# A hybrid decoder step: input rows turned once, the roots multiplied in by feature tile, conditioning and weight blocks loaded between input tiles, and a tile's halves overlapped

## The reference, cut to what matters

```python
mod = jax.nn.silu(c) @ w_ada + b_ada
sh1, sc1, g1, sh2, sc2, g2 = (m[:, None, :] for m in jnp.split(mod, 6, axis=-1))
h = rmsnorm(x, norm_mix_w) * (1.0 + sc1) + sh1
z = h @ w_in + b_in
q_raw, f_raw, i_raw, og_raw, glu_a, glu_b, gate_a, gate_b = jnp.split(z, IN_SPLITS, axis=-1)
```

## Time and profile before

| | |
|---|---|
| median of 3 runs | 1977.72 us (1976.07 to 1977.74) |
| the profiled execution's own time | 1975.14 us |
| its span, first to last instruction | 1973.4 us |
| busy share of the span: TensorE, VectorE, ScalarE, GpSimd | 98%, 67%, 33%, 12% |
| mean granted clock of TensorE | 0.994 of full |
| moved from and to memory | 237.45 MB, 120 GB/s over the span |

### The profile page before, as it was taken

How to read it: one execution, slowest core, us unless ns; L and a number is a source line. 1 busy time by engine, 2 the same in 40 slices (tenths; PEclk the granted TensorE clock), 3 DMA queues, 4 the chain that set the end, 5 groups by cost and what they waited for, 6 DMA issues and landing times.

```text
span 1973.4 us, 39636 instructions
## 1 busy us (share of the span) xinstructions
PE 1935.4 (98%) x16182; PEld 1876.1 (95%) x16182; DVE 1316.6 (67%) x1800; ACT 655.9 (33%) x1066; POOL 232.5 (12%) x256
## 2 busy tenths in 40 slices
PE   7999999999999999998999999999999999999998
PEld 6999999999999999988989999999999999999998
DVE  6697979786878788897775665554445544465543
ACT  6212313131413222233544433333343333433332
POOL 2300000000000000021132554700000000000000
PEclk8999999999999999999999999999999999999999
DMA  8723041413232222222366644444444544444443
GB/s 254 229 61 87 24 112 45 112 45 92 66 90 67 70 77 79 78 75 93 107 216 210 187 135 139 132 138 140 136 137 143 154 136 136 135 147 148 138 133 110
DMA packets 417245, 237.45 MB, mean 120 GB/s; under 512 B 16375, under 2 KB 411287, under 8 KB 417072
## 3 DMA queue, kind: packets, MB, share of 16 engines
q1 hardware_dynamic: 416672, 234.48, 40.6%
q10 hardware_dynamic: 416, 0.72, 0.1%
HBM read 211.91 MB, written 24.11 MB: 120 GB/s over the span
## 4 chain that ended last, share of the span: by engine, by line
PE 83%; DVE 10%; ACT 3%; issue 2%; DMA 1%; DVEq 0%; POOL 0%; ACTq 0%; SPq 0%
PE Z L887 45%; PE Z L905 27%; DVE yb L1453 4%; DVE w_lo L1305 2%; PE R L980 1%; PE Z L852 1%; PE R L924 1%; ACT w_hi L1813 1%; PE R L1006 1%; PE R L930 1%; PE R L1013 1%; PE R L1015 1%; PE R L987 1%; DVE S L1420 1%; DMA w_raw<-in_w_out_dram 1%
## 5 line engine op out<-in xcount | busy, mean ns | idle before, releaser
L1813 ACT ACTIVATE w_hi<-w_raw 128x1024 fp32r<-128x1024 f32 (+1 forms) x316 | 329.4, 1043 | 932.3 <-PE Z L887 469.7
L1305 DVE TENSOR_TENSOR w_lo<-w_raw,w_hi 128x1024 fp32r<-128x1024 f32 (+1 forms) x305 | 386.0, 1266 | 369.1 <-ACT w_hi L1813 361.4
L905 PE MATMUL Z<-h_hi,w_hi 128*128 128x352 f32 x1488 | 499.7, 336 | 2.8 <-issue 1.7
L905 PE MATMUL Z<-h_hi,w_lo 128*128 128x352 f32 x1488 | 478.4, 321 | 0.0
L905 PE MATMUL Z<-h_lo,w_hi 128*128 128x352 f32 x1488 | 477.8, 321 | 0.0
L1453 DVE SCALAR_TENSOR_TENSOR yb<-up,vec,yb 128x1024 f32 (+1 forms) x240 | 327.2, 1363 | 28.8 <-DVE yb L1453 3.7
L887 PE MATMUL Z<-h_hi,w_hi 128*128 128x352 f32 x1056 | 342.1, 324 | 0.0
L887 PE MATMUL Z<-h_hi,w_lo 128*128 128x352 f32 x1056 | 339.2, 321 | 0.0
L887 PE MATMUL Z<-h_lo,w_hi 128*128 128x352 f32 x1056 | 338.6, 321 | 0.0
L905 PEld LDWEIGHTS Z<-h_hi,w_hi 128*128 128x128 f32 x1488 | 279.5, 188 | 20.2 <-issue 16.7
L905 PEld LDWEIGHTS Z<-h_lo,w_hi 128*128 128x128 f32 x1488 | 280.3, 188 | 0.5 <-issue 0.5
(11 more groups left out here) (303 smaller groups left out, 2408.8 us busy)
## 6 DMA issues: line engine op xcount, KB each, us to landing
w_raw<-in_w_ffn_in_dram SPq DMA_DIRECT2D x132, 512.0 KB, 3.8
w_raw<-in_w_in_dram SPq DMA_DIRECT2D x64, 512.0 KB, 5.0
w_raw<-in_w_out_dram SPq DMA_DIRECT2D x48, 512.0 KB, 4.2
w_raw<-in_w_ffn_out_dram SPq DMA_DIRECT2D x48, 512.0 KB, 4.0
aw<-in_w_ada_dram SPq DMA_DIRECT2D x32, 512.0 KB, 4.0
w_raw<-in_w_ffn_out_dram SPq DMA_DIRECT2D x24, 384.0 KB, 3.4
ada_w<-in_w_ada_dram SPq DMA_DIRECT2D x16, 512.0 KB, 6.2
mbuf<-merged_scratch SPq DMA_DIRECT2D x32, 176.0 KB, 4.3
```

The costliest lines, as they stand in the source:

```text
L905: last = mm(out, w[:, kt, :], x[:, kt, cols], start=kt == 0 and m == 0, stop=kt == NJ - 1 and m == 2)
L1305: st.tell(V.tensor_tensor(w_lo[b.par][:, 0:n, :], w_raw[b.par][:, 0:n, :], w_hi[b.par][:, 0:n, :].bitcast(F32), ALU.subtract), w_split, b. ...
L1813: A(w_hi[b.par][:, 0:n, :], w_raw[b.par][:, 0:n, :], ACT.Copy).then_inc(w_hi_ready, 1)
```

## The change

The roots are no longer multiplied into the rows before turning. The input is turned once, as it is; the root of each token is spread over all partitions by one small matmul per row tile (`root_row`) and kept as `rsrow` (128 x 1056), and the scaling is `xt * am * rsrow` by feature tile. The nine row tiles have a buffer each, where h_hi comes later. The copies of the turned x pass from ScalarE to VectorE. SyncE's queue has block 0, x4, conditioning 0, x5, block 1, x6, conditioning 1, x7, x8, and then conditioning 2 to 7 in four buffers. Conditioning 0 and 1 are made between the turns. In the tile loop the prompt part of h is made in two halves of 512 tokens by VectorE (scale), ScalarE (h_hi with the shift as bias) and VectorE (h_lo); the 32 sample tokens go to GpSimd. `conditioning(kt + 2)` moves behind block 0's products of tile kt, `fold_groups(kt + 2)` into block 1's. The last two tiles are made for block 0 first and then for block 1. The exponentials of the lower bounds move from the input phase into the loop.

TensorE:

```diff
+                for t in range(NC + 1):
+                    turn_tokens(t)
+                    if t >= 2:
+                        root_row(t - 2)
+                    if t == 2:
+                        vectors()
+                    if t == 4:
+                        conditioning(0)
+                    if t == 5:
+                        pe.wait_ge(const_ready, 3)
+                        fold_groups(0)
+                    if t == 7:
+                        conditioning(1)
+                for t in range(NC - 1, NC + 1):
+                    root_row(t)
+                fold_groups(1)
                 pe.wait_ge(x_evac, N_TURNS)
...
+                pe.wait_ge(row_copied, NC + 1)
+                pe.wait_ge(w_split, 2)
+                for kt, b in FIRST_STEPS:
+                    pe.wait_ge(h_ready, kt + 1)
+                    pe.wait_ge(hs_ready, kt + 1)
+                    for m, (w, x) in enumerate(((w_hi[b], h_hi), (w_hi[b], h_lo), (w_lo[b], h_hi))):
+                        for g in range(G):
+                            last = mm(Z[b][:, g, 0:GW], w[:, kt, :], x[:, kt, g * GW:(g + 1) * GW],
+                                      start=kt == 0 and m == 0, stop=kt == NJ - 1 and m == 2)
+                        if b == 1 and m == 1 and kt + 2 < NJ:
+                            fold_groups(kt + 2)
+                    if kt == NJ - 1:
+                        last.then_inc(block_done, 1)
+                    if b == 0 and kt + 2 < NJ:
                         conditioning(kt + 2)
...
+            def root_row(t):
+
+                m = tokens(t)
+                pe.wait_ge(rms_ready, t + 1)
+                wait(pe, row_copied, t - 2)
+                mm(row_bank(t), rs9[0:m, t:t + 1].to_broadcast([m, P]), ident[0:m, 0:m], start=True, stop=True) \
+                    .then_inc(row_made, 1)
```

```diff
+FIRST_STEPS = tuple((kt, b) for kt in range(NJ - 2) for b in range(2)) + tuple(
+    (kt, b) for b in range(2) for kt in range(NJ - 2, NJ))
+HALF_PROMPT = (slice(0, TP // 2), slice(TP // 2, TP))
```

VectorE (after the copies of xt and of the rows; `condition(0)` stands behind t = 7):

```diff
+            def scale_prompt(j):
                 st.settle()
...
+                for half in HALF_PROMPT:
+                    st.tell(V.scalar_tensor_tensor(hbuf[j % 3][:, half], xt[:, j, half], am[:, j, 0:1], rsrow[:, half],
+                                                   ALU.mult, ALU.mult), h_full, 2 * j + 1 + HALF_PROMPT.index(half))
+
+            def prompt_low(j):
+
+                for n, half in enumerate(HALF_PROMPT):
+                    dve.wait_ge(h_hi_ready, 2 * j + n + 1)
+                    ins = V.scalar_tensor_tensor(h_lo[:, j, half], hbuf[j % 3][:, half], mod[:, SH1 * NJ + j, 0:1],
+                                                 h_hi[:, j, half].bitcast(F32), ALU.add, ALU.subtract)
+                    st.do(ins) if n == 0 else st.tell(ins, h_ready, j + 1)
...
+                if j:
+                    condition(j)
+                scale_prompt(j)
+                prompt_low(j)
+                if j == 2:
+                    lower_bounds_in()
+                if j == 5:
+                    lower_bounds()
+            dve.wait_ge(hs_ready, NJ)
```

ScalarE:

```diff
+            def groups_out(j):
+                act.wait_ge(ada_done, j + 1)
+                A(acols[:, j % 2, :, :].rearrange("p s n -> p (s n)"), R[j % 2][:, 0:2 * P], ACT.Copy).then_inc(acols_ready, 1)
...
+                if t in (5, 8):
+                    groups_out(t // 8)
+                if t in (3, 5):
+                    hi(Idx(t // 4))
+
+            for j in range(NJ):
+                for n, half in enumerate(HALF_PROMPT):
+                    act.wait_ge(h_full, 2 * j + n + 1)
+                    A(h_hi[:, j, half], hbuf[j % 3][:, half], ACT.Identity, bias=mod[:, SH1 * NJ + j, 0:1]) \
+                        .then_inc(h_hi_ready, 1)
+                if j + 2 < NJ:
+                    groups_out(j + 2)
+                if j == 3:
                     act.wait_ge(lb_in, 1)
                     A(lbs[:, 0, :], lbs[:, 0, :], ACT.Exp)
                     A(lbs[:, 1, :], lbs[:, 1, :], ACT.Exp).then_inc(lb_exp, 1)
```

GpSimd (the splits of blocks 0 and 1 now stand ahead of the roots of row tiles 4 and 6):

```diff
+            pool.wait_ge(row_copied, NC + 1)
+            pool.wait_ge(x_evac, N_TURNS)
+            st.tell(Q.tensor_tensor(xs[:, :, :], xt[:, :, TP:T], rsrow[:, TP:T].unsqueeze(1).to_broadcast([P, NJ, TS]),
+                                    ALU.mult), xs_scaled, 1)
+
+            def samples(j):
+
+                pool.wait_ge(am_ready, j + 1)
...
+                st.do(Q.tensor_tensor(seqs(xs[:, j, :]), seqs(xs[:, j, :]), per_seq(am[:, j, 1:NSEQ]), ALU.mult))
+                st.settle()
+                st.do(Q.tensor_tensor(seqs(h_hi[:, j, TP:T]), seqs(xs[:, j, :]), shift, ALU.add))
+                st.do(Q.tensor_tensor(seqs(full), seqs(xs[:, j, :]), shift, ALU.add))
+                st.settle()
+                st.tell(Q.tensor_tensor(h_lo[:, j, TP:T], full, h_hi[:, j, TP:T].bitcast(F32), ALU.subtract),
+                        hs_ready, j + 1)
```

More of the change, by code:

```diff
@@ L325, in program @@
     ada_w = [e(f"ada_w{i}", [P, 2, 8, P]) for i in range(WADA)]
-    xrow = [e(f"xrow{i}", [P, D]) for i in range(XBUF)]
     vrow = e("vrow", [P, 4, P])
+    rsrow = e("rsrow", [P, T])
+    xs, hs = e("xs", [P, NJ, TS]), e("hs", [P, NJ, TS])
     hbuf = (ta, tb, ysum)
@@ L521, in load_mod @@
                         .then_inc(adaw_loaded[j % WADA], 16)
-            for t in range(XBUF):
+            for t in range(4):
                 load_x(t)
@@ L788, in vectors, with turn_tokens @@
                 last.then_inc(p0_done, 1)
-            def turn(t, row, normed, done, read):
+            def turn_tokens(t):
+                pe.wait_ge(x_loaded[t], 16)
                 m = tokens(t)
                 for n in range(2 * t, 2 * t + 2):
-                    wait(pe, read, n - 2)
-                    bank = turn_bank(normed, n)
+                    wait(pe, x_evac, n - 2)
+                    bank = turn_bank(n)
                     for j in range(4):
[L797 to L812, removed]
+                        c = (4 * (n % 2) + j) * P
+                        last = transpose(bank[:, j * m:(j + 1) * m], xrow[0:m, t, c:c + P], ident[0:m, 0:m])
+                    last.then_inc(x_turned, 1)
+            def root_row(t):
[4 more added lines that the diff above has]
+                    .then_inc(row_made, 1)
             def conditioning(j):
@@ L1251, in lower_bounds, with copy_row, condition @@
                 st.do(V.tensor_scalar(lbs[:, 2, :], lbs[:, 0, :], 1.0, None, ALU.subtract))
[L1253 to L1277, removed]
+            def copy_row(t):
+                dve.wait_ge(row_made, t + 1)
+                st.tell(V.tensor_copy(rsrow[:, t * P:t * P + tokens(t)], row_bank(t)), row_copied, t + 1)
+            def condition(j):
                 dve.wait_ge(folded, j + 1)
-                st.do(add_bias(SH1))
-                st.tell(add_bias(SC1), mod_read, j + 1)
+                made = R[j % 2][:, FOLD_COL:FOLD_COL + 32].rearrange("p (s n) -> p s n", n=16)[:, :, 0:NSEQ]
+                bias = vec[:, V_ADA:V_ADA + 6 * NJ].rearrange("p (s j) -> p s j", j=NJ)[:, SH1:SC1 + 1, j:j + 1]
+                st.tell(V.tensor_tensor(mod[:, :, :].rearrange("p (s j) n -> p s j n", j=NJ)[:, SH1:SC1 + 1, j, :], made,
+                                        bias.to_broadcast([P, 2, NSEQ]), ALU.add), mod_read, j + 1)
                 st.settle()
@@ L1293, in modulate @@
-                dve.wait_ge(h_hi_ready, j + 1)
-                st.tell(V.tensor_tensor(h_lo[:, j, :], buf[:, 0:T], h_hi[:, j, :].bitcast(F32), ALU.subtract), h_ready,
-                        j + 1)
-            for j in range(NJ):
-                modulate(j)
+            for t in range(NC + 1):
+                for n in range(2 * t, 2 * t + 2):
+                    dve.wait_ge(x_turned, n + 1)
+                    st.tell(V.tensor_copy(turned(xt, n), turn_bank(n)[:, 0:4 * tokens(t)].rearrange(
+                        "p (j t) -> p j t", j=4)), x_evac, n + 1)
+                if t >= 2:
+                    copy_row(t - 2)
+                if t == 3:
+                    first_evac(1, vec[:, :], R[1][:, 0:NVEC])
+                if t == 7:
+                    condition(0)
@@ L2133, in _ @@
                         rms_ready, t + 1)
-            for b in range(2):
-                low(Idx(b))
+            pool.wait_ge(row_copied, NC + 1)
[4 more added lines that the diff above has]
+                pool.wait_ge(am_ready, j + 1)
+                if j == 0:
+                    pool.wait_ge(xs_scaled, 1)
+                full, shift = hs[:, j, :], per_seq(mod[:, SH1 * NJ + j, 1:NSEQ])
+                st.do(Q.tensor_tensor(seqs(xs[:, j, :]), seqs(xs[:, j, :]), per_seq(am[:, j, 1:NSEQ]), ALU.mult))
[5 more added lines that the diff above has]
+                        hs_ready, j + 1)
+            for j in range(NJ):
+                samples(j)
             pool.wait_ge(h_ready, NJ)
```

92 lines of the change are left out of this document (26 added, 66 removed).

## The result

| | before | changed |
|---|---|---|
| median, us | 1977.73 (1976.07 to 1978.03, 6 runs) | 1988.57 (1986.22 to 1990.04, 6 runs) |
| ratio, 95% interval | | 1.0057 [1.0046, 1.0068] |
| span of the profiled execution, us | 1973.4 | 1986.8 |
| block 2 starts, us | 74.84 | 84.80 |
| mean granted clock | 0.994 | 0.992 |

A forecast was written before the change was run, and what follows sets the result against it. TensorE was taken to bound the kernel, so only the start-up counts: block 2 moves from 74.84 to 79.7 us (37.2 + 7.0 + 20.8 + 6.7, then 3.6, 1.5, 2.9), +4.9 on the median: 1982.6 us, range 1975.5 to 1986.5.

The forecast's parts named there:

- Part 2: Tile loop: ScalarE's queue order closes a loop through conditioning, 5.2 us a tile where TensorE's own work is 4.57.
- Rival C: Tile loop: ScalarE's queue doesn't bind and TensorE paces it as before; -2.6 us, 1975.1 us; chance 0.13.
- four times 5.2, and once 5.2 + 1.5: Tile loop from T(1) to T(6): four tiles of 5.2 us and one of 6.7 with table load and Exp.
- Nine more products end block 0 at 76.8: Loop's end: after T(7) at 75.3, block 0 ends at 76.8 and block 2 starts 2.9 later, at 79.7 us.
- Part 1: Input phase until T(0): x7 lands at 28.0 us, last copies end at 33.6, T(0) follows at 37.2.
- T(0): Moment when tile 0's first product can start, forecast at 37.2 us.
- rival B: Input phase: TensorE is at 2.4 GHz when x7 lands and at T(0); +0.9 us, 1978.6 us; chance 0.28.
- Rival D: Tile 0, loop and T(7): every GpSimd sample operation lands whole in VectorE's time; +3.1, 1985.7 us; chance 0.11.
- Part 3: Loop's end, from T(6) at 71.7 to block 2 at 79.7 us, with the 1.1 us stall for split weights gone.
- T(6) to T(7): From tile 6's first possible product to tile 7's: VectorE begins h(7) only at T(6), 3.6 us.

The follow-up runs named there:

- e1: Changed kernel with conditioning(kt+2) put ahead of tile kt's products again; 1978.29 us, ratio to before 1.0009.
- e7: Changed kernel's tile loop and Exp with e6's input phase (all input tiles loaded before the weights); 1981.64 us, ratio to before 1.0029.
- e3: Changed kernel with 18 unread matmuls put on TensorE into each gap, ahead of tile 4 and of tile 7's block 0 products; 1987.09 us, ratio to before 1.0053.
- e10: Changed kernel with GpSimd's sample operations held until VectorE has finished h_lo of the same tile; one execution, 2003.94 us.
- e5: Changed kernel with e1 and e2 together and the fold between a tile's two blocks as before the change; 1976.51 us, ratio to before 1.0002.
- e6: e5 with all inputs loaded before weights, conditionings 0 and 1 behind all turns, block 0 and 1 splits on VectorE; 1972.78 us, ratio to before 0.9990.
- e4: Changed kernel with blocks 0 and 1 alternating in the last two tiles as well, as before the change; 1988.03 us, ratio to before 1.0057.
- e2: Changed kernel with the two Exp and their table load moved back into the input phase; 1985.46 us, ratio to before 1.0048.

## Why the prediction was right about the sign and wrong about the size

**Part 2, the loop through ScalarE's queue: right.** Forecast 5.2 us a tile, measured 5.31, 5.30 and 5.28 for the undisturbed tiles; e1 shows the cause. The sum was right by terms that partly were not: I had two halves of h_hi and one low half on the chain (1.2 + 0.69 and two semaphores), and the chain shows one h_hi half and both low halves (0.62 + 1.43); nine products are 1.72, not 1.6. Rival C (TensorE paces the loop) fell: what follows the conditioning was not inside TensorE's remaining work.

**The step that failed** is in parts 2 and 3: "four times 5.2, and once 5.2 + 1.5" and "Nine more products end block 0 at 76.8 ... Block 2 starts at 76.8 + 2.9". Both price TensorE's work behind a gap at the higher clock. I had charged the low clock to the gaps of the input phase, which the trace of before shows, and not to the two gaps that the change itself opens. The runs show 1.5 us behind the first (6.77 instead of 5.3: 3.01 for nine products and 1.24 for the conditioning, against 1.71 and 1.05) and 1.75 behind the second (6.15 instead of 4.4), of which the clock has 1.54 (4.61 in e7, behind a like gap at the full clock). With e3 filling them, both go.

**Part 1: mis-sized by 1.3.** T(0) was forecast at 37.2 and came at 38.51. Of it 1.0 is the load of x7: its square starts at 29.02, not 28.0. I divided only the bytes queued ahead of x7 by the saturated rate; the trace has 284 GB/s over the first 29.0 us, 8.24 MB, so 5.86 MB moved after the first 10 us (2.38 MB at 238 GB/s), 0.62 MB more than the 5.24 counted. The surplus fits transfers queued behind x7 that share the rate with it: x7 was under way from 19.98 to 29.00, x8 and conditioning 2 were issued from 22.80 and 23.27 on. No run separates this. TensorE was at the lower clock for turn 7, 1.97 us, as forecast; rival B fell. That the work from there to the last row copy came out nearly right (5.69 us against 5.6) is luck: conditioning 1 took 1.45 instead of 1.9 and the small turns 0.61 instead of 0.8, since the clock rose in between, and the rows took 1.42 instead of 0.5. The halves with GpSimd beside them took 3.78 from the last row copy against 3.6.

**Rival D, the shared port:** there, and smaller than priced. The forecast had 0.8 at tile 0 and D 0.9 more; e10 shows 0.56 in all, and later tiles lose 0.08 (the pair takes 1.50 instead of 1.42), outside the chain but for tile 7.

**Part 3:** T(6) to T(7) 3.49 against 3.6, and no wait for w_lo at block 2, as forecast.

The misses add up: T(0) 1.31; the plain tiles 0.38 (7.09 against 7.0, and 5.31, 5.30, 5.28 against 5.2); the tile of the Exp 0.20 (6.90 against 6.7); the tile behind it 1.57; T(6) to T(7) -0.11; the end 1.75; together 5.10 = 84.80 - 79.7. That leaves 10.8 - 10.0 = 0.8 us behind block 2 (nothing, if it is counted from the second trace of before, where block 2 starts 0.9 earlier). The stretch from block 2 to the recurrence stage's last products takes 920.0 and 920.1 us in the two traces of before and 921.0 to 922.0 in all eleven traces of the changed kernel and what was made from it. It gathers slowly: w_hi splits of the same blocks stand 9.72 us later than before at 283 us, 10.0 at 403, 10.4 at 644 and 10.8 at 762. So about 1 to 2 us do come from there, in every kernel with the new start. The cause stays open; no run was made for it.

## What to carry to other kernels

An operation that one engine owes to another must not stand in that engine's queue behind one that waits for the other's newest result: here h_hi(j+1) stood behind a copy of groups that were made only after tile j's products, and 0.7 us a tile and all slack went with two moved lines. When a change opens a gap on TensorE, charge the gap and then the work behind it at the lower clock; the second was here nearly as large as the first (1.5 behind gaps of 2.08 and 1.78), though not every gap brought it. And when the last input decides, load it first: taking weights out from ahead of the inputs gave 5.9 us at T(0) and, between e5 and e6, 3.7 in the median, more than any mending of the operations did apart from the queue.

## What the runs showed of the hardware that was not expected

- The clock fell behind gaps of 2.08 us and 1.78 us in a TensorE that was busy 9.06 of the 10 us from 50 us on. The gap of 2.08 brought it down wherever it was left open in a 5.3 us loop (changed, e4, e7), and the one of 1.78 did in the changed kernel and e2 (6.15, 6.16). One of 1.77 in e7 and one of 1.65 in e1 did not (4.61 both), nor did 1.73 and 1.59 in e10. So near 1.8 us these traces do not tell ahead whether it falls, and what decides it stays open.
- Extra matmuls whose results nobody reads made the loop 2.7 us shorter (46.3 to 43.6, one trace each).
- T(0) of kernels with the same order of loads spread from 37.95 to 40.26 us (changed, e1 to e5; e2 and e5 also have the Exp in the input phase), by when x7 lands (turn 7 starts at 28.57 to 29.71) and at which clock TensorE works from there. Between the changed kernel, e3 and e4, whose input phases are the same line for line, it is 1.75 us that no edit explains.
